# Two small transformers in one kernel: the activation areas of the matmuls placed 64 bytes short of the weight tiles modulo 256, and the low activation product issued last in the second network

## The chip, the cores and the metric

The kernel runs on one core of one Trainium2 chip. The metric is the device time of one execution in microseconds (us); the median of three executions is quoted. One profiled execution gives the trace that all durations come from. The engines in it are TensorE (PE for matmuls, PEld for weight loads), VectorE (DVE), ScalarE (ACT), GpSimd (POOL) and SyncE (SP, which issues the DMAs).

## The reference

Two networks of two layers each are computed one after the other, in fp32, on 256 tokens of 1024 features. The first has 256 more tokens of context, which its first layer carries and its second drops. The second network puts 16 learned tokens in front, so it works on 272.

```
# first network, one layer (cut)
hx = modulate(rmsnorm(x, norm1_g[l]), shift, scale)
p  = hx @ w_in[l]                       # conv branch | q k v | two gates
x  = x + gate * gated_merge(p[..., QKV_END:], conv_branch(...), attention(...), w_out[l])
x  = x + gate * conv_ffn(modulate(rmsnorm(x, norm2_g[l]), ...), w_up[l], ffn_dw[l], ffn_dw_b[l], w_down[l])
# second network, one layer (cut)
u = rmsnorm_2(h, norm_mix[l]);  proj = u @ w_in[l]
h = h + concatenate([a_out, b_out, c_out]) @ w_out[l]      # sparse, differential and retention attention
u = rmsnorm_2(h, norm_ff[l]);   h = h + square(relu(u @ w_ff1[l])) @ w_ff2[l]
```

## The kernel before

All activations live in SBUF, features on the 128 partitions and tokens along the free axis. Every weight is read from HBM once, as a stream of 442 slabs of 128 x 1024 numbers (512 KB). A slab holds 8 tiles of 128 x 128.

**A weight's way.** SP loads slab i into `raw`, a ring of four (`RING`); ScalarE rounds it to fp32r into `w_hi` (line 846); GpSimd writes the rest, raw minus `w_hi`, into `w_lo` in two halves (line 803). SP may load slab i+4 once `w_lo` of slab i is written; ScalarE may round slab i+4 once TensorE has finished slab i. The first network uses `w_hi0`/`w_lo0`, the second `w_hi1`/`w_lo1` over the same bytes; in the second, each pair of tiles starts 64 bytes further than the one before (`TURN` = 16 numbers), so tile k starts 64k bytes further modulo 256.

**A product.** An fp32 product is made of three fp32r matmuls for each tile: high weights by high activations (line 1369), high weights by low activations (line 1370), low weights by high activations (line 1374). The weights are the stationary operand, loaded by a LDWEIGHTS of 128 columns before every matmul, and the activations (`h`, `y`, `at`, `cv`, `fa`, `dn` in the first network; `v`, `u`, `o`, `f` in the second, each as a `_hi` and a `_lo` area) are the moving one: 512 columns in the first layer, 256 in the second layer of the first network, 272 or 256 in the second network. A slab is 24 such matmuls. In `chunk` and in the up projection of the first network all 16 products with `w_hi` come first and the 8 with `w_lo` after them; in the second network the order is high-high, high-low, low-high for each tile. Some products have the weights as the moving operand (lines 1657 to 1659, 1966 to 1968 and 2081 to 2083; two runs of 256 columns each).

**Where the areas start.** The weight tiles start at byte 32896 of a partition. The table gives the start of the moving area relative to that, modulo 256, and how it goes on from one 128-feature tile k to the next.

| area | before | of tile k |
|---|---|---|
| `h`, `y`, `at`, `cv`, `dn` | 0 | same for all k, as are the weights |
| `as`, `cs` (second layer's `at`, `cv`), `fa` | 192 | same for all k, as are the weights |
| `v`, `u`, `o`, `f` with 272 columns | 192, high and low alike | 64k further, as are the weights |
| `u` of the second layer, 256 of its columns (the first 16 left out) | 64 | 64k further, as are the weights |
| `o` of the second layer, 256 columns | 192 | 64k further, as are the weights |

**The up projection of the second layer of the first network** matters below. Its 22 pairs of slabs (`up`, lines 1067, 1752 and 2612) run in loops on all engines. For pair j TensorE makes the `a` chunk and the `g` chunk; ScalarE scales each out of its bank (`up_a`, `up_g`, line 1088), VectorE adds two taps to each (line 2258), ScalarE takes a tanh (`up_t`, line 1093), VectorE makes the product and puts it back into the bank of the `g` chunk (line 2250), ScalarE rounds that into `fa_hi` (line 856) and VectorE writes the rest to `fa_lo`. Between these ScalarE rounds the coming weight slabs. TensorE may write the bank of `g` chunk j only when `fa_lo` of pair j-2 is written (`up_split`).

Of the kernel before, what the change touches and what calls it, by code (L numbers as in the profile page):

```python
# [18 lines left out]
F32 = mybir.dt.float32  # L19
# [93 lines left out]
_n = 0  # L113
for _name, _w in (("ident", P), ("ones_d", P), ("ones_c", P), ("ones_h", P), ("perm1", P), ("perm2", P),
                  ("sel", 8), ("hsel", 16), ("sums", 2), ("cos1", SEQ), ("sin1", SEQ), ("win", GRID_W),
                  ("cos2", T2), ("sin2", T2), ("causal", N1 + N2), ("decay", 4 * 512),
                  ("onehot", VLEN), ("vmask", VLEN)):
    TAB[_name] = (_n, _n + _w)
    _n += _w
# [7 lines left out]
def build(nc, A, out, marks):  # L127
# [44 lines left out]
    with ctx:  # L172
# [28 lines left out]
        w_lo = [weight_area(f"w_lo{n}", w_at + w_size, turn) for n, turn in enumerate((0, TURN))]  # L201
        cst = sb("cst", [6 * P + 26])
        prm = sb("prm", [DEPTH, PRM1_N])
# [67 lines left out]

        def shifted(name, rows, o, by):
            return at(name, [rows, T_BOTH], F32R, o + by)[:, :, 0:SEQ]
# [20 lines left out]
        assert 192 + 3 * DC * T2 * 4 + 4096 <= 2 * DC * T_BOTH * 4  # L294
        tab2 = at("tab2", [2 * T2 + N1 + N2 + 4 * 512], F32, x_at)
# [13 lines left out]
        o_hi = at("o_hi", [DC, T2], F32R, o)  # L309
        o_lo = at("o_lo", [DC, T2], F32R, o + DC * T2 * 4)  # L310
        v_lo = at("v_lo", [DC, T2], F32R, o)
        v_hi = at("v_hi", [DC, T2], F32R, o + DC * T2 * 4)
        units = [(o_hi, o_lo), tuple(at(f"o_{part}1", [DC, T2], F32R, o + 192 + n * DC * T2 * 4) for n, part in enumerate(("hi", "lo")))]
        o += 2 * DC * T2 * 4 + 192
        bias2 = at("bias2", [A_HEADS + B_HEADS, S_ALL], F32, o)
# [6 lines left out]
        assert o + 1536 + 3 * T2 * 4 <= end1, (o, end1)  # L322
        assert g_at + 192 + 2 * FF2_C * T2 * 4 <= o

# [17 lines left out]
        ident = cst[:, 0:P]  # L342
        ones_d, ones_c, ones_h = (cst[:, i * P:(i + 1) * P] for i in (1, 2, 3))
        perm1, perm2, sel = cst[:, 4 * P:5 * P], cst[:, 5 * P:6 * P], cst[:, 6 * P:6 * P + 8]
        hsel = cst[:, 6 * P + 8:6 * P + 24]
        sums = cst[:, 6 * P + 24:6 * P + 26]

# [486 lines left out]
        def _(act):  # L834
# [90 lines left out]
            def network1(layer):  # L925
# [27 lines left out]
                def attend(kind, n, *others):  # L953
# [32 lines left out]
                    elif kind == "mean":  # L986
                        for c in range(CONV_C):
                            act.wait_ge(*after("conv_centred", (layer, c)))
                            act.activation(conv_sq(c)[:, 0:T], cv[:, c, 0:T], ACT.Square).then_inc(*done("ln_sq", (layer, c)))
                    elif kind == "V":  # L990
                        act.wait_ge(*after("attn_pv", (layer, n)))
                        copy(attns[layer][0][:, n, 0:T], aux[3][:, 0:T]).then_inc(*done("attn_hi", (layer, n)))
                    elif kind == "var":

                        ahead(s + 2 * DC)
# [48 lines left out]
                for c in range(CONV_C + 1):  # L1044
# [3 lines left out]
                    if c:  # L1048
                        act.wait_ge(*after("conv_silu", (layer, c - 1)))
                        copy(convs[layer][0][:, c - 1, 0:T], nb[:, c - 1, 0:T]).then_inc(*done("conv_hi", (layer, c - 1)))  # L1050

# [294 lines left out]
        def _(pe):  # L1346
# [29 lines left out]
            def three(o, i, k, a_hi, a_lo, start, stop):  # L1376

                two(o, i, k, a_hi, a_lo, start)
                return third(o, i, k, a_hi, stop)

            def chunk(i, b, T, a_hi, a_lo, key, reader, h_key=None, t0=0):
# [4 lines left out]
                for k in range(DC):  # L1386
                    if h_key:
                        pe.wait_ge(*after("norm_lo", (h_key, k)))
                    two(bank[b][:, t0:T], i, k, a_hi[:, k, t0:T], a_lo[:, k, t0:T], k == 0)
                    if not late:  # L1390
                        mm = third(bank[b][:, t0:T], i, k, a_hi[:, k, t0:T], k == DC - 1)
                if late:
# [201 lines left out]
            def network1(layer):  # L1594
# [108 lines left out]
                def attention_branch(m):  # L1703
# [4 lines left out]
                    for k in range(4):  # L1708
                        three(bank[m % 4][:, 0:T], s + m, 4 + k, attns[layer][0][:, k, 0:T], attns[layer][1][:, k, 0:T], k == 0, k == 3)

                def conv_branch(m):
                    b = 4 + m % 4
                    claim(b)
                    for k in range(4):
                        if m == 0:
                            pe.wait_ge(*after("conv_lo", (layer, k)))
                        mm = three(bank[b][:, 0:T], s + m, k, convs[layer][0][:, k, 0:T], convs[layer][1][:, k, 0:T], k == 0, k == 3)
                    mm.then_inc(*done("slab_used", s + m))
# [529 lines left out]
        def _(dve):  # L2248
# [137 lines left out]
            def network1(layer):  # L2386
# [106 lines left out]
                def rest(p):  # L2493

                    dve.wait_ge(*after("attn_hi", (layer, p)))
                    tt(attns[layer][1][:, p, 0:T], aux[3][:, 0:T], attns[layer][0][:, p, 0:T].bitcast(F32), ALU.subtract)\
                        .then_inc(*done("attn_lo", (layer, p)))
# [51 lines left out]
                for c in range(CONV_C + 2):  # L2549
# [10 lines left out]
                    if c >= 2:  # L2560
                        dve.wait_ge(*after("conv_hi", (layer, c - 2)))
                        tt(convs[layer][1][:, c - 2, 0:T], nb[:, c - 2, 0:T], convs[layer][0][:, c - 2, 0:T].bitcast(F32), ALU.subtract)\
                            .then_inc(*done("conv_lo", (layer, c - 2)))
# [446 lines left out]
def shape_tables():  # L3010
# [9 lines left out]
    put("ones_c", np.full((P, P), 1 / (CONV_C * P)))  # L3020
    put("ones_h", (i[:, None] // HD == i[None, :] // HD) / HD)
    for name, half in (("perm1", 16), ("perm2", 32)):
# [190 lines left out]
```

## Time and profile before

| | |
|---|---|
| median of three executions | 1959.35 us (1958.83 to 1960.12) |
| span of the profiled execution | 1959.9 us |
| TensorE matmuls | 1904.2 us busy (97%), 12126 of them |
| weight loads | 1624.1 us busy (83%) |
| GpSimd | 1187.7 us (61%) |
| VectorE | 1065.5 us (54%) |
| ScalarE | 891.8 us (46%) |
| DMA | 307.04 MB, mean 157 GB/s |
| granted TensorE clock | 9 of 10 tenths or more in all 40 slices |

The span runs from the first to the last instruction. A matmul's duration in the records (277 to 400 ns) is longer than the distance to the next one's start, since they are pipelined: the time that a stream of matmuls takes is read from start to start. Times of rows below are in us from the span's start unless marked ns.

### The profile page before, as it was taken

Reading aid. Unit: us, or ns where it says so; the run is one execution under the profiler, and the core shown is the slowest. Engines: PE = TensorE matmul, PEld = TensorE weight load, DVE = VectorE, ACT = ScalarE, POOL = GpSimd, SP = SyncE. Lnnn points to the kernel's source line nnn. Section 1 sums busy time; section 2 is a strip of 40 time slices with the busy share of each in tenths; the row PEclk is TensorE's granted clock in tenths of the full one; section 3 lists DMA queues with packets and bytes.
Section 4 is the critical chain, followed back from the end, with each engine's and each line's share of the span. In section 5 each row is a group of like instructions: output and inputs, shape, how many; then the busy total and the mean of one; then the engine's idle time right before and its main releaser. Section 6 shows DMA issues by size and latency. Waiting matters only on the chain.

```text
span 1959.9 us, 33261 instructions
## 1 busy us (share of the span) xinstructions
PE 1904.2 (97%) x12126; PEld 1624.1 (83%) x12126; DVE 1065.5 (54%) x1972; ACT 891.8 (46%) x1520; POOL 1187.7 (61%) x904
## 2 busy tenths in 40 slices
PE   7999999999999999999899999999999999999998
PEld 4677777888888887877889999787999998769987
DVE  4899865354443324887657744876542048555400
ACT  4223444243443323525546645556554355555533
POOL 2444233424654554635469987674788876649986
PEclk9999999999999999999999999999999999999999
DMA  9942233628433343436465575432455564326554
GB/s 387 362 127 76 56 96 117 228 78 172 147 107 107 120 149 121 150 91 211 139 204 172 182 230 182 164 108 89 130 183 182 173 206 139 109 75 205 185 179 130
DMA packets 121541, 307.04 MB, mean 157 GB/s; under 512 B 29640, under 2 KB 51528, under 8 KB 121044
## 3 DMA queue, kind: packets, MB, share of 16 engines
q1 hardware_dynamic: 118808, 300.98, 46.8%
q10 hardware_dynamic: 2620, 4.51, 1.5%
q8 instruction: 77, 1.26, 0.3%
q14 instruction: 36, 0.29, 0.0%
HBM read 300.72 MB, written 8.06 MB: 158 GB/s over the span
## 4 chain that ended last, share of the span: by engine, by line
issue 36%; POOL 31%; PE 28%; DVE 4%; ACT 1%; POOLq 0%; ACTq 0%; DVEq 0%
POOL w_lo L803 30%; PE bank L1369 7%; PE bank L1374 6%; PE bank L1370 6%; PE bank L2081 2%; PE bank L2082 2%; PE bank L2083 2%; DVE nb L2258 1%; PE bank L1966 1%; PE bank L1968 1%; PE bank L1967 1%; ACT w_hi L846 0%; DVE v_lo L2258 0%; PE bank L2185 0%; DVE v_lo L2250 0%
## 5 line engine op out<-in xcount | busy, mean ns | idle before, releaser
L803 POOL TENSOR_TENSOR w_lo<-raw,w_hi 128x512 fp32r<-128x512 f32 x884 | 1169.7, 1353 | 759.4 <-ACT w_hi L846 757.2
L846 ACT ACTIVATE w_hi<-raw 128x1024 fp32r<-128x1024 f32 x442 | 466.1, 1056 | 285.2 <-PE bank L1374 146.8
L1369 PE MATMUL bank<-h_hi,w_hi 128*128 128x256 f32 (+1 forms) x1248 | 407.4, 342 | 1.8 <-DVE h_lo L2258 1.1
L1370 PE MATMUL bank<-h_lo,w_hi 128*128 128x256 f32 (+1 forms) x1248 | 399.4, 336 | 0.0
L1369 PEld LDWEIGHTS bank<-h_hi,w_hi 128*128 128x128 f32 x1248 | 237.2, 190 | 43.0 <-issue 13.2
L1374 PE MATMUL bank<-h_hi,w_lo 128*128 128x256 f32 (+1 forms) x1248 | 262.8, 335 | 0.0
L1370 PEld LDWEIGHTS bank<-h_lo,w_hi 128*128 128x128 f32 x1248 | 237.3, 190 | 23.6 <-issue 0.2
L1374 PEld LDWEIGHTS bank<-h_hi,w_lo 128*128 128x128 f32 x1248 | 204.7, 190 | 23.9
L1369 PE MATMUL bank<-u_hi,w_hi 128*128 128x272 f32 (+1 forms) x736 | 212.0, 288 | 1.1 <-DVE u_lo L2258 1.1
L1374 PE MATMUL bank<-u_hi,w_lo 128*128 128x272 f32 (+1 forms) x736 | 209.1, 284 | 0.0
L1370 PE MATMUL bank<-u_lo,w_hi 128*128 128x272 f32 (+1 forms) x736 | 208.3, 283 | 0.0
L1369 PEld LDWEIGHTS bank<-u_hi,w_hi 128*128 128x128 f32 x736 | 138.7, 188 | 5.5 <-issue 3.6
L1370 PEld LDWEIGHTS bank<-u_lo,w_hi 128*128 128x128 f32 x736 | 138.9, 189 | 0.1
L1374 PEld LDWEIGHTS bank<-u_hi,w_lo 128*128 128x128 f32 x736 | 138.9, 189 | 0.0
L2258 DVE SCALAR_TENSOR_TENSOR cv<-upad,prm,cv 128x512 f32<-128x512 f32 x120 | 129.0, 1075 | 3.6
L2258 DVE SCALAR_TENSOR_TENSOR up_g<-bank,prm,up_g 128x510 f32<-128x510 f32 (+1 forms) x88 | 54.2, 616 | 82.4 <-ACT up_g L1088 76.3
L2258 DVE SCALAR_TENSOR_TENSOR up_a<-bank,prm,up_a 128x510 f32<-128x510 f32 (+1 forms) x88 | 54.1, 614 | 56.4 <-ACT up_a L1088 50.4
L2250 DVE TENSOR_TENSOR bank<-bank,sq 128x272 f32<-128x272 f32 (+1 forms) x76 | 33.4, 440 | 93.3 <-ACT up_t L1296 93.2
L1369 PE MATMUL bank<-f_hi,w_hi 128*128 128x272 f32 x256 | 73.8, 288 | 0.0
L1374 PE MATMUL bank<-f_hi,w_lo 128*128 128x272 f32 x256 | 73.8, 288 | 0.0
L2258 DVE SCALAR_TENSOR_TENSOR X<-bank,gh,X 128x256 f32<-128x256 f32 x48 | 21.6, 479 | 95.3 <-PE bank L1374 95.3
L1370 PE MATMUL bank<-f_lo,w_hi 128*128 128x272 f32 x256 | 72.9, 285 | 0.0
(394 smaller groups left out, 3720.8 us busy)
## 6 DMA issues: line engine op xcount, KB each, us to landing
raw<-in_wstream SPq DMA_DIRECT2D x442, 512.0 KB, 3.5
ada_raw<-in_wada SPq DMA_DIRECT2D x48, 512.0 KB, 13.1
late_a<-in_wada SPq DMA_DIRECT2D x16, 512.0 KB, 5.1
late_b<-in_wada SPq DMA_DIRECT2D x16, 512.0 KB, 4.5
biash<-rpb_by_offset SPq DMA_DIRECT2D x64, 64.0 KB, 2.5
gates<-in_wada SPq DMA_DIRECT2D x8, 512.0 KB, 5.0
rpb_by_offset<-in_rpb SPq DMA_DIRECT2D x16, 224.0 KB
bias_by_distance<-vec ACTq DMA_DIRECT2D x1, 3264.0 KB
```

Of the source, the lines that this page charges most:

```text
L803: i = pool.tensor_tensor(lo[:, part, s, :], whole[:, part, :], hi[:, part, s, :].bitcast(F32), ALU.subtract)
L846: act.activation(w_hi[q >= first["l2", 0]][:, :, s, :], raw[:, s, :].rearrange("p (g c) -> p g c", c=PAIR), ACT.Copy)\
L1369: pe.matmul(o, tile(w_hi, i, k), a_hi, start=start, stop=False)
L1370: pe.matmul(o, tile(w_hi, i, k), a_lo, start=False, stop=False)
L1374: return pe.matmul(o, tile(w_lo, i, k), a_hi, start=False, stop=stop)
L1966: pe.matmul(lin[b][:, :], a, wh, start=kk == 0, stop=False)
L1967: pe.matmul(lin[b][:, :], al, wh, start=False, stop=False)
L2081: pe.matmul(o[:, :], hi, wh, start=j == 0, stop=False)
L2082: pe.matmul(o[:, :], lo, wh, start=False, stop=False)
L2083: return pe.matmul(o[:, :], hi, wl, start=False, stop=j == FF2_C - 1)
L2250: return dve.tensor_tensor(o, a, b, op)
L2258: return dve.scalar_tensor_tensor(out=o, in0=a, scalar=s, in1=b, op0=op0, op1=op1)
```

## The change

The activation areas are placed so that they start 64 bytes short of the weight tiles modulo 256 (192 in the table above). `h`, `y`, `at` and `cv` move from 0 to 192; `fa`, and the second layer's `at` and `cv`, which had shifted copies for it, stay at 192. `dn` stays at 0. In the second network the high areas stay at 192 (`u` of the second layer moves so that the 256 columns start at 192 and the 272 at 128), and every low area starts 64 bytes further than its high one, at 0. There the three products of a tile come as high-high, low-high, high-low. An unused table of constants (`ones_h`, 512 bytes of a partition) goes, which makes room. `qT`, `kT`, `gates`, `ada_raw`, `pj` and `V2`, which lie in the same bytes or behind them, move along by 192 bytes modulo 256.

```diff
@@
         X = sb("X", [DC, T_BOTH])
+        top[0] += (w_at - 64 - top[0]) % 256
         h_at = top[0]
@@
-        fa_hi = at("fa_hi", [FF_C, SEQ], F32R, g_at + 192)
-        fa_lo = at("fa_lo", [FF_C, SEQ], F32R, g_at + 192 + FF_C * SEQ * 4)
+        fa_hi = at("fa_hi", [FF_C, SEQ], F32R, g_at)
+        fa_lo = at("fa_lo", [FF_C, SEQ], F32R, g_at + FF_C * SEQ * 4)
@@
-        top[0] += (128 - top[0]) % 256
+        top[0] += (w_at - 64 - top[0]) % 256
         cv_at = top[0]
@@
-        attns = [(at_hi, at_lo), (shifted("as_hi", QC, q_at, 192), shifted("as_lo", QC, q_at + QC * T_BOTH * 4, 192))]
-        convs = [(cv_hi, cv_lo), (shifted("cs_hi", CONV_C, up_at, 192), shifted("cs_lo", CONV_C, cv_at, 192))]
@@
-        o += 192
-        ffn_in = [tuple(at(f"u_{part}{l}", [DC, T2], F32R, o + by + n * DC * T2 * 4) for n, part in enumerate(("hi", "lo")))
-                  for l, by in enumerate((0, -192))]
+        low_part = DC * T2 * 4 + 64
+        ffn_in = [tuple(at(f"u_{part}{l}", [DC, T2], F32R, o + by + n * low_part) for n, part in enumerate(("hi", "lo")))
+                  for l, by in enumerate((0, 192))]
+        o += 256
@@
-        ffn_mid = [tuple(at(f"f_{part}{l}", [FF2_C, n_mid], F32R, o + by + n * FF2_C * n_mid * 4) for n, part in enumerate(("hi", "lo")))
-                   for l, (n_mid, by) in enumerate(((T2, 192), (SEQ, 0)))]
+        ffn_mid = [tuple(at(f"f_{part}{l}", [FF2_C, n_mid], F32R, o + by + n * (FF2_C * n_mid * 4 + 64)) for n, part in enumerate(("hi", "lo")))
+                   for l, (n_mid, by) in enumerate(((T2, 0), (SEQ, 64)))]
@@
             def three(o, i, k, a_hi, a_lo, start, stop):
 
-                two(o, i, k, a_hi, a_lo, start)
-                return third(o, i, k, a_hi, stop)
+                if i < first["l2", 0]:
+                    two(o, i, k, a_hi, a_lo, start)
+                    return third(o, i, k, a_hi, stop)
+                pe.matmul(o, tile(w_hi, i, k), a_hi, start=start, stop=False)
+                pe.matmul(o, tile(w_lo, i, k), a_hi, start=False, stop=False)
+                return pe.matmul(o, tile(w_hi, i, k), a_lo, start=False, stop=stop)
```

The order changes on TensorE alone, in the second network alone. The place below is the end of the first feed-forward projection and the start of the second in its first layer. Before:

```order
L1369 MATMUL bank<-u_hi_111,w_hi_51 128x272
L1370 MATMUL bank<-u_lo_112,w_hi_51 128x272
L1374 MATMUL bank<-u_hi_111,w_lo_53 128x272
L2053 REGISTER_ALU
L2053 COMPARE_AND_BRANCH
L1369 MATMUL bank<-f_hi_123,w_hi_51 128x272
L1370 MATMUL bank<-f_lo_124,w_hi_51 128x272
L1374 MATMUL bank<-f_hi_123,w_lo_53 128x272
```

The same place in the changed kernel:

```order
L1378 MATMUL bank<-u_hi_107,w_hi_51 128x272
L1379 MATMUL bank<-u_hi_107,w_lo_53 128x272
L1380 MATMUL bank<-u_lo_108,w_hi_51 128x272
L2055 REGISTER_ALU
L2055 COMPARE_AND_BRANCH
L1378 MATMUL bank<-f_hi_119,w_hi_51 128x272
L1379 MATMUL bank<-f_hi_119,w_lo_53 128x272
L1380 MATMUL bank<-f_lo_120,w_hi_51 128x272
```

The product with the low activations went from second to third place; nothing was added or taken away.

## Rows read from the trace of the kernel before

**Rows 1.** The page's first section: busy time, share and instructions of each engine.

```profile
PE 1904.2 (97%) x12126; PEld 1624.1 (83%) x12126; DVE 1065.5 (54%) x1972; ACT 891.8 (46%) x1520; POOL 1187.7 (61%) x904
```

**Rows 2.** Groups by line and shape, TensorE: shape, count | busy us, mean ns | idle before.

```profile
L1369 PE MATMUL bank<-h_hi,w_hi 128*128 128x512 f32 x608 | 243.3, 400 | 0.0
...
L1369 PE MATMUL bank<-h_hi,w_hi 128*128 128x256 f32 x640 | 164.2, 287 | 1.8 <-DVE h_lo L2258 1.1 <-ACT V L856 0.8
...
L1369 PE MATMUL bank<-u_hi,w_hi 128*128 128x272 f32 x416 | 121.2, 291 | 0.3 <-DVE u_lo L2258 0.3
...
L1369 PE MATMUL bank<-u_hi,w_hi 128*128 128x256 f32 x320 | 90.9, 284 | 0.8 <-DVE u_lo L2258 0.8
...
L1369 PE MATMUL bank<-f_hi,w_hi 128*128 128x272 f32 x256 | 73.8, 288 | 0.0
```

**Rows 3.** Timeline, TensorE, up projection of layer one: start, duration, what.

```profile
601.73 0.39 PE L1369 MATMUL bank<-h_hi,w_hi 128*128 128x512 f32 x1
...
605.13 0.39 PE L1370 MATMUL bank<-h_lo,w_hi 128*128 128x512 f32 x1
```

**Rows 4.** Timeline, TensorE and VectorE, up projection of layer two, near its end.

```profile
1135.75 0.28 PE L1369 MATMUL bank<-h_hi,w_hi 128*128 128x256 f32 x1
...
1137.43 1.12 PE L1374 MATMUL bank<-h_hi,w_lo 128*128 128x256 f32 x8
1137.46 0.41 DVE L2250 TENSOR_TENSOR fa_lo<-bank,fa_hi 128x256 f32 x1
...
1138.39 0.28 PE L1369 MATMUL bank<-h_hi,w_hi 128*128 128x256 f32 x1
```

**Rows 5.** Timeline, TensorE, attention and convolution outputs of layer two.

```profile
978.02 0.28 PE L1369 MATMUL bank<-as_hi,w_hi 128*128 128x256 f32 x1
...
981.76 0.28 PE L1369 MATMUL bank<-cs_hi,w_hi 128*128 128x256 f32 x1
```

**Rows 6.** Timeline, TensorE, second feed-forward projection of the second network, 272 columns.

```profile
1499.83 0.29 PE L1374 MATMUL bank<-f_hi,w_lo 128*128 128x272 f32 x1
...
1503.18 0.29 PE L1374 MATMUL bank<-f_hi,w_lo 128*128 128x272 f32 x1
```

**Rows 7.** Timeline, TensorE, output projection, last layer, 256 columns.

```profile
1764.94 0.28 PE L1369 MATMUL bank<-o_hi,w_hi 128*128 128x256 f32 x1
...
1767.78 0.28 PE L1369 MATMUL bank<-o_hi,w_hi 128*128 128x256 f32 x1
```

**Rows 8.** Timeline, TensorE, first feed-forward projection, last layer, 256 columns.

```profile
1789.91 0.28 PE L1369 MATMUL bank<-u_hi,w_hi 128*128 128x256 f32 x1
...
1793.07 0.28 PE L1369 MATMUL bank<-u_hi,w_hi 128*128 128x256 f32 x1
```

**Rows 9.** Timeline, TensorE, last feed-forward projection, weights as moving operand.

```profile
1900.18 0.40 PE L2082 MATMUL bank<-w_hi,f_lo 128*128 128x512 f32 x1
1900.42 0.39 PE L2083 MATMUL bank<-w_lo,f_hi 128*128 128x512 f32 x1
...
1904.85 0.40 PE L2081 MATMUL bank<-w_hi,f_hi 128*128 128x512 f32 x1
```

**Rows 10.** Instructions on the tile fa_lo, 1016 to 1150: durations ns, first and last start.

```profile
L2250 DVE TENSOR_TENSOR fa_lo<-bank,fa_hi x21: 411/415/417, 1032.9 to 1148.9; 128x256 f32 x20, 128x256 fp32r<-128x256 f32 x1
```

**Rows 11.** All waits of ScalarE, 1016 to 1147: us in total, times, longest.

```profile
ACT up_t L1093 <- DVE up_g L2258: 26.0, 20, 1.8
ACT fa_hi L856 <- DVE bank L2250: 16.2, 10, 1.8
ACT h_hi L922 <- DVE nb L2258: 3.8, 6, 2.4
ACT up_a L1088 <- PE bank L1374: 3.2, 1, 3.2
```

**Rows 12.** Longest wait of TensorE in the attention of layer two, 800 to 960.

```profile
PE bank L1891 <- DVE sq L2254: 4.5, 6, 1.0
```

More of the change, by code:

```diff
@@ L113 @@
 _n = 0
-for _name, _w in (("ident", P), ("ones_d", P), ("ones_c", P), ("ones_h", P), ("perm1", P), ("perm2", P),
+for _name, _w in (("ident", P), ("ones_d", P), ("ones_c", P), ("perm1", P), ("perm2", P),
                   ("sel", 8), ("hsel", 16), ("sums", 2), ("cos1", SEQ), ("sin1", SEQ), ("win", GRID_W),
@@ L305, in build @@
         V2 = at("V2", [3, 1024], F32, o + L2_FRONT * T2 * 4)
-        ffn_mid = [tuple(at(f"f_{part}{l}", [FF2_C, n_mid], F32R, o + by + n * FF2_C * n_mid * 4) for n, part in enumerate(("hi", "lo")))
-                   for l, (n_mid, by) in enumerate(((T2, 192), (SEQ, 0)))]
+        ffn_mid = [tuple(at(f"f_{part}{l}", [FF2_C, n_mid], F32R, o + by + n * (FF2_C * n_mid * 4 + 64)) for n, part in enumerate(("hi", "lo")))
+                   for l, (n_mid, by) in enumerate(((T2, 0), (SEQ, 64)))]
         o += (L2_FRONT * T2 + 3 * 1024) * 4
[L309 to L314, printed above, removed]
+        o += (w_at - 64 - o) % 256
+        units = [tuple(at(f"o_{part}{l}", [DC, T2], F32R, o + by + n * low_part) for n, part in enumerate(("hi", "lo")))
+                 for l, by in enumerate((0, 192))]
+        v_lo = at("v_lo", [DC, T2], F32R, o + 64)
+        v_hi = at("v_hi", [DC, T2], F32R, o + 256 + DC * T2 * 4)
+        o += 2 * DC * T2 * 4 + 256
         bias2 = at("bias2", [A_HEADS + B_HEADS, S_ALL], F32, o)
@@ L342, in build @@
         ident = cst[:, 0:P]
[L343 to L346, printed above, removed]
+        ones_d, ones_c = (cst[:, i * P:(i + 1) * P] for i in (1, 2))
+        perm1, perm2, sel = cst[:, 3 * P:4 * P], cst[:, 4 * P:5 * P], cst[:, 5 * P:5 * P + 8]
+        hsel = cst[:, 5 * P + 8:5 * P + 24]
+        sums = cst[:, 5 * P + 24:5 * P + 26]
         by_distance = nc.dram_tensor("bias_by_distance", (A_HEADS + B_HEADS, P, VLEN), F32).ap()
@@ L991, in attend @@
                         act.wait_ge(*after("attn_pv", (layer, n)))
-                        copy(attns[layer][0][:, n, 0:T], aux[3][:, 0:T]).then_inc(*done("attn_hi", (layer, n)))
+                        copy(at_hi[:, n, 0:T], aux[3][:, 0:T]).then_inc(*done("attn_hi", (layer, n)))
                     elif kind == "var":
@@ L1049, in network1 @@
                         act.wait_ge(*after("conv_silu", (layer, c - 1)))
-                        copy(convs[layer][0][:, c - 1, 0:T], nb[:, c - 1, 0:T]).then_inc(*done("conv_hi", (layer, c - 1)))
+                        copy(cv_hi[:, c - 1, 0:T], nb[:, c - 1, 0:T]).then_inc(*done("conv_hi", (layer, c - 1)))
                 for m in range(DC):
@@ L1388, in chunk @@
                         pe.wait_ge(*after("norm_lo", (h_key, k)))
-                    two(bank[b][:, t0:T], i, k, a_hi[:, k, t0:T], a_lo[:, k, t0:T], k == 0)
-                    if not late:
-                        mm = third(bank[b][:, t0:T], i, k, a_hi[:, k, t0:T], k == DC - 1)
+                    if late:
+                        two(bank[b][:, t0:T], i, k, a_hi[:, k, t0:T], a_lo[:, k, t0:T], k == 0)
+                    else:
+                        mm = three(bank[b][:, t0:T], i, k, a_hi[:, k, t0:T], a_lo[:, k, t0:T], k == 0, k == DC - 1)
                 if late:
@@ L1708, in attention_branch @@
                     for k in range(4):
-                        three(bank[m % 4][:, 0:T], s + m, 4 + k, attns[layer][0][:, k, 0:T], attns[layer][1][:, k, 0:T], k == 0, k == 3)
+                        three(bank[m % 4][:, 0:T], s + m, 4 + k, at_hi[:, k, 0:T], at_lo[:, k, 0:T], k == 0, k == 3)
                 def conv_branch(m):
@@ L1716, in conv_branch @@
                             pe.wait_ge(*after("conv_lo", (layer, k)))
-                        mm = three(bank[b][:, 0:T], s + m, k, convs[layer][0][:, k, 0:T], convs[layer][1][:, k, 0:T], k == 0, k == 3)
+                        mm = three(bank[b][:, 0:T], s + m, k, cv_hi[:, k, 0:T], cv_lo[:, k, 0:T], k == 0, k == 3)
                     mm.then_inc(*done("slab_used", s + m))
@@ L2495, in rest @@
                     dve.wait_ge(*after("attn_hi", (layer, p)))
-                    tt(attns[layer][1][:, p, 0:T], aux[3][:, 0:T], attns[layer][0][:, p, 0:T].bitcast(F32), ALU.subtract)\
+                    tt(at_lo[:, p, 0:T], aux[3][:, 0:T], at_hi[:, p, 0:T].bitcast(F32), ALU.subtract)\
                         .then_inc(*done("attn_lo", (layer, p)))
```

11 lines of the change are left out of this document (4 added, 7 removed).

## The prediction

> **What bounds the kernel now.** I read the page's first section first [rows 1]: TensorE is busy for 97% of the span and no other engine for more than 61%, so the time is made by the stream of matmuls, and its pace is what counts. Since durations overlap, I then read the pace from start to start, in the timeline, at places where nothing waits:
>
> - 512 columns, `h`: 15 steps from 601.73 to 605.13, 226.7 ns each [rows 3].
> - 256 columns, `h`: 22 steps (14, and then the 8 of the last row but one) from 1135.75 to 1138.39, 120.0 ns each [rows 4].
> - 256 columns, `as` and `cs`: 33 steps from 978.02 to 981.76, 113.3 ns each [rows 5].
> - 272 columns, `f`: 27 steps from 1499.83 to 1503.18, 124.1 ns each [rows 6].
> - 256 columns, `o` of the last layer: 24 steps from 1764.94 to 1767.78, 118.3 ns [rows 7]; `u` of the last layer: 27 steps from 1789.91 to 1793.07, 117.0 ns [rows 8].
>
> Four paces for one size of matmul. `as` and `h` have the same columns, the same row length and the same weights; by the code they differ in where the area starts. What fits all rows is the distance between two streams that run together: while matmul n streams its activation columns, the weights of matmul n+1 are loaded (both engines' rows are busy side by side, 97% and 83% [rows 1]). Let d be the start of those weights minus the start of the streaming activations, modulo 256. One column at the full 2.4 GHz level makes 106.7 ns of 256 columns, so what is paid on top is:
>
> - d = 0 always (`h`): 13.3 ns a matmul.
> - d = 64 always (`as`, `cs`): 6.6 ns.
> - d = 64, 64, 128 (`o`; the third matmul of a tile is followed by the next tile's weights, 64 bytes further): three steps are 354.9 ns, and two of them at 113.3 leave 128.3 for the third, so d = 128 costs 21.6 ns.
> - d = 192, 192, 0 (`u` of the last layer): 117.0 on average.
> - 272 columns (113.3 ns of streaming), d = 64, 64, 128: 10.8 ns on average; by the costs above it would be (6.6 + 6.6 + 21.6) / 3 = 11.6. So the columns hardly matter, the distances do. And 512 columns (213.3 ns) at d = 0 pay 13.4, as 256 do.
>
> **The change part by part.** It makes d = 64 nearly everywhere. The counts are those of line 1369 [rows 2], times three for the three products; smaller groups of the same view are told with their count.
>
> First network, 512 columns: `h` 608, `y` 64, `at` 32, `cv` 32, together 736, or 2208 matmuls. No row has 512 columns with the activations moving at d = 64. The bounds are no gain and 13.4 ns (all that is paid now); I take 6.7, because at d = 0 the cost is the same 13.3 at either width and at 256 columns half of it goes [rows 3 to 5]. 2208 x 6.7 = 14.8 us. `dn` (504 matmuls) stays at 0 and gains nothing.
>
> First network, 256 columns: `h` 640 and `y` 64, or 2112 matmuls, from 120.0 to 113.3: 14.2 us at full price.
>
> Second network, 272 columns: `u` 416 (of which 48 are the second layer's), `f` 256, `v` 120, `o` 64; without those 48 it is 808, or 2424 matmuls. The new order and the 64 bytes of the low areas turn 64, 64, 128 into 64, 64, 64: after low-high come the same tile's high weights, and the last product streams the low area, which starts 64 further, so the next tile's weights are again 64 ahead. The step would be 113.3 + 6.6 = 119.9 against 124.1: 2424 x 4.2 = 10.2 us. Bounds: nothing, and 10.8 ns (26 us).
>
> Second network, 256 columns: `u` 320, or 960 matmuls, from 117.0 to 113.3, 3.6 us; `o` 64, or 192, from 118.3, 1.0 us.
>
> Small ones, taken together as nothing: the second layer's 144 matmuls of `u` with 272 columns get d = 128 throughout where they had 0, 0, 64 (144 x 10 ns, 1.5 us lost); where the weights move (lines 1657, 1966, 2081) the stationary activations shift, and in 128 of them d goes from 0 or 128 to 64 or 192 (about 9 ns each, 1.2 us won). The attention products on `qT`, `kT`, `pj` and `V2` are true fp32 and have no low parts; I count their 192 bytes at nothing, with a loss of 1 us as the far bound. The new order itself costs nothing: `w_lo` was waited for at the start of a chunk before as well, a weight load stands before each matmul either way, and no other engine's order moves. GpSimd, ACT and DMA get 4% less time for a slab in places: all of GpSimd's 1187.7 us over 442 slabs are 2.69 us a slab [rows 1], against 2.72 for 24 steps of 113.3. In the down projection of layer two TensorE already runs at that pace with `fa`.
>
> Sum at full price: 14.8 + 14.2 + 10.2 + 4.6 = 43.8 us.
>
> **What takes its place.** In the up projection of layer two TensorE makes a pair of slabs in 48 x 120.0 = 5.76 us. `fa_lo`, the last step of each pair on the other engines, starts 21 times from 1032.9 to 1148.9: 116.0 / 20 = 5.80 us a pair [rows 10]. That is slower than TensorE, and it isn't TensorE that makes it so: in this stretch ScalarE waits 42.2 us for VectorE and once, at the start, for TensorE [rows 11]. Scaling, taps, tanh, product, rounding and the coming weight slab make a ring of ScalarE and VectorE that turns on its own. TensorE needs `fa_lo` of two pairs back for its bank; near the end that is written at 1137.87 and needed at 1138.39 [rows 4], 0.5 us of slack. Faster matmuls use up the slack and then wait in step with the ring. There 40 slabs x 24 = 960 of the 2112 matmuls lie, worth 6.4 us; 0.5 stays, 5.9 goes.
>
> In the attention of both layers, TensorE waits for the softmax (six times, 4.5 us, in layer two [rows 12]). Of the gate chunks between a pair's scores and its transposes the gain is swallowed by a longer wait: 8 slabs a layer at 24 x 6.7 ns, 1.3 us each, most of it in layer two: 2 us. The starts of stages (norms, the first loads in the first 50 us) take 2 us more, an estimate from the loose steps there. Together 9.9 us are lost of 43.8, and 33.9 us are left. The profiled span is 1959.9, half a us over the median of 1959.35, so nothing lies outside it; the forecast is 1959.35 - 33.9 = **1925.5 us**, 1.7% less.
>
> **A rule that speaks against it.** The rows show one matmul shape at 120.0 and at 113.3 ns with only the area's start changed [rows 4, 5]. The Trainium skill, "SBUF — State Buffer", section "SBUF: two separate sides", says that on the engine side only the pair of ports shared by VectorE and GpSimd causes contention and that TensorE waits for no one; "TensorE: Matmul & The Clock Gate", Part 2, gives the moving operand and the weight load a read port each, so that one takes no bandwidth from the other. By that the start of an area can't matter and the change would be worth nothing.
>
> **The rivals.** (a) Placement isn't the cause, and `as`, `cs` and `fa` are fast for a reason that goes with their stages: 1959, no change. Against it: `f`, `o` and `u` have three more paces, and the distances alone put all of them in order. 4%. (b) At 512 columns the cost doesn't fall, since the load is over halfway through the matmul, and what is paid isn't the meeting of two streams but a start-up: 14.8 less, 1940. For it: no row with 512 at 64. Against it: the equal 13.3 at 256. 12%. (c) The second network keeps 124, because the 64-distance there was never alone: 10.2 less, 1936. 12%, and 2% for (b) and (c) together, 1950. (d) The ring in the up projection isn't as fixed as it looks; its product on VectorE takes 0.4 or 1.4 us, as it meets GpSimd or not, and with other phases it may turn in less than 5.76: up to 5.9 more, and the attention's 2, 1917. 7%. (e) Slower: the 512-column matmuls fall on a worse place instead of a better. With the weights moving, 512-column steps take 233.5 on average (20 steps, 1900.18 to 1904.85) and single ones 240 [rows 9]. Without the 14.8 the rest is worth 19.1; it is gone when the 2208 lose 8.7 ns each, at a step of 235.4. At 240 the sum is 1959 - 19 + 29, so 1969. 3%.
>
> **How the numbers follow.** The forecast case, 1925.5, has 60%; (a) 4, (b) 12, (c) 12, both 2, (d) 7, (e) 3. Its own working bounds are some 5 us either way (the swallowed part, and 1 to 2 ns on 2424 matmuls). To leave out no more than 20% the range takes in (b), (c) and (d): 1914 to 1943. 0.2% (4 us) is about what a measurement of this kernel can tell from no change. Faster by more: all but (a), (e), with a little off for both together: 0.93; within: 0.04; slower: 0.03.
>
> **What would show it.** In the changed kernel's timeline: steps of 220 ns with `h` at 512 columns (226.7 means b); 113.3 with `h` at 256 outside the up projection of layer two; in that stage about 5.8 us a pair, with TensorE waiting for `fa_lo`, and ScalarE still not waiting for TensorE; 120 at 272 columns in a slab of 2.88 us (124 means c); 113.3 for `u` and `o` of the last layer; `dn` still at 227. What would make the prediction wrong is above all the width of 512, 14.8 of the 33.9, and a GpSimd that doesn't keep up at 2.72 us a slab where the ring of four starts empty.

## The result: 0.6% slower, and the profile after

The changed kernel takes 1972.39 us (median of 4 runs, 1970.29 to 1974.56) beside 1959.57 for the kernel before, a ratio of 1.0062 with a 95% interval of 1.0051 to 1.0074. Forecast were 1925.5, and 1943 at most. In a second comparison, ten runs beside nineteen of before, the ratio was 1.0054 (1.0039 to 1.0069). All ratios here compare executions in the chip's usual, faster state; one of an experiment below, 3123.58 us at a mean granted clock of 0.555, is left out by that. The profiled execution spans 1971.2 us where that of before spans 1959.9.

The page's first section and one of its groups. TensorE has 12.7 us more of busy time than in [rows 1], with the same number of instructions; VectorE, ScalarE and GpSimd are within 1.1 us of it:

```profile
PE 1916.9 (97%) x12126; PEld 1623.0 (82%) x12126; DVE 1064.4 (54%) x1972; ACT 891.5 (45%) x1520; POOL 1187.0 (60%) x904
...
L1366 PE MATMUL bank<-h_hi,w_hi 128*128 128x256 f32 (+1 forms) x1248 | 409.0, 344 | 3.6 <-DVE fa_lo L2252 1.7
```

The timeline answers to [rows 3], the up projection of layer one with 512 columns. From 602.02 to 605.29 are 14 steps (4, the 8 low products, 2), 233.6 ns each, where 220 was forecast and 226.7 was before:

```profile
602.02 0.40 PE L1366 MATMUL bank<-h_hi,w_hi 128*128 128x512 f32 x1
...
602.96 2.03 PE L1371 MATMUL bank<-h_hi,w_lo 128*128 128x512 f32 x8
604.82 0.40 PE L1366 MATMUL bank<-h_hi,w_hi 128*128 128x512 f32 x1
605.06 0.39 PE L1367 MATMUL bank<-h_lo,w_hi 128*128 128x512 f32 x1
605.29 0.40 PE L1366 MATMUL bank<-h_hi,w_hi 128*128 128x512 f32 x1
```

Layer two, 256 columns, the same lines and tiles at two places (answers to [rows 4]). From 1059.89 to 1063.89 are 34 steps of 117.6 ns; from 1099.84 to 1100.98 are 10 of 114. In between and behind stand waits for `fa_lo`, and after one of them the other pace is there:

```profile
1059.89 0.28 PE L1366 MATMUL bank<-h_hi,w_hi 128*128 128x256 f32 x1
...
1063.89 0.28 PE L1366 MATMUL bank<-h_hi,w_hi 128*128 128x256 f32 x1
...
1099.84 0.28 PE L1366 MATMUL bank<-h_hi,w_hi 128*128 128x256 f32 x1
...
1100.98 1.07 PE L1371 MATMUL bank<-h_hi,w_lo 128*128 128x256 f32 x8
1102.48 0.39 PE L1366 MATMUL bank<-h_hi,w_hi 128*128 128x256 f32 x1 [0.44 <-DVE fa_lo L2252]
```

The second network, answers to [rows 6] and [rows 8]: 272 columns, 30 steps from 1515.05 to 1518.83, 126.0 ns (124.1 before); `u` of the last layer, 30 steps from 1800.03 to 1803.48, 115.0 ns (117.0 before).

```profile
1515.05 0.29 PE L1378 MATMUL bank<-f_hi,w_hi 128*128 128x272 f32 x1
...
1518.83 0.29 PE L1378 MATMUL bank<-f_hi,w_hi 128*128 128x272 f32 x1
...
1800.03 0.28 PE L1378 MATMUL bank<-u_hi,w_hi 128*128 128x256 f32 x1
...
1803.48 0.28 PE L1378 MATMUL bank<-u_hi,w_hi 128*128 128x256 f32 x1
```

Where the time went is read from the first start of some tiles. The answers for single tiles (durations min/median/max, first and last start), first of before, then of the changed kernel:

```profile
L1369 PE MATMUL bank<-dn_hi,w_hi x168: 387/389/467, 656.1 to 775.2; 128*128 128x512 f32 x168
L1369 PE MATMUL bank<-fa_hi,w_hi x176: 276/276/384, 1147.0 to 1207.1; 128*128 128x256 f32 x176
L1369 PE MATMUL bank<-f_hi,w_hi x256: 287/288/290, 1496.6 to 1591.7; 128*128 128x272 f32 x128
L2081 PE MATMUL bank<-w_hi,f_hi x128: 390/395/478, 1861.4 to 1953.9; 128*128 128x512 f32 x128
```

```profile
L1366 PE MATMUL bank<-dn_hi,w_hi x168: 387/389/467, 666.4 to 785.6; 128*128 128x512 f32 x168
L1366 PE MATMUL bank<-fa_hi,w_hi x176: 276/276/384, 1157.0 to 1218.6; 128*128 128x256 f32 x176
L1378 PE MATMUL bank<-f_hi,w_hi x256: 283/288/289, 1510.1 to 1606.6; 128*128 128x272 f32 x128
L2083 PE MATMUL bank<-w_hi,f_hi x128: 388/395/482, 1872.5 to 1965.1; 128*128 128x512 f32 x128
```

The lag, by which the same instruction starts later in the changed kernel, is 10.3 us at the start of `dn` (nearly all of it 512-column work), 11.5 at the start of `y` in layer two (986.4 and 997.9, rows below), 10.0 at the start of `fa` and 11.5 at its end, 13.5 at the start of `f` and 14.9 at its end, 11.1 at the last projection, 11.3 at the end of the span. So the first 650 us lose nearly all, the rest of the first network loses 1.2 more, the 272-column layer takes 3.4, and the last one gives 3.8.

**The clock has a share in this.** Both traces have short stretches in which TensorE is granted 1.2 GHz, and the changed kernel's has one more, in the attention of layer two, right after TensorE had waited 1.79 us for `qT`. The answer for this stretch (0.50, the third number from the end, is the granted share of the full 2.4 GHz; before has 1.00 in this part):

```profile
827.90:831.30 3.40, 3.40 (x17) 3.31 (x16) 2.65 (x7) 1.69 (x3) 3.40 (x4) 0.50 0.57 163
```

In it 15 matmuls of 256 columns start, where at 117.8 ns there would be 29: 1.6 us of the lag. The mean granted clock of the two profiled executions is 0.994 and 0.991. Over the 82 runs of before on record, 0.001 less of it goes with about 1.2 us more (a straight line through them, an estimate), and the 14 runs of the changed kernel have 0.9937 on average where those have 0.9947. So some 1 to 2 of the 10 to 13 us go with the clock; whether the change brings that about wasn't tested.

### The profile page after: what moved, and what is told of

Same layout as the page of the kernel before. It is cut to its first block, busy times and chain, and to the rows that moved or that the text cites. A ratio compares the mean times of both kernels' runs of the same rounds, so it can differ in the third digit from the quotient of the medians.

```text
span 1971.2 us, 33261 instructions
## 1 busy us (share of the span) xinstructions
PE 1916.9 (97%) x12126; PEld 1623.0 (82%) x12126; DVE 1064.4 (54%) x1972; ACT 891.5 (45%) x1520; POOL 1187.0 (60%) x904
## 4 chain that ended last, share of the span: by engine, by line
issue 37%; POOL 30%; PE 29%; DVE 3%; ACT 1%; POOLq 0%; DMA 0%; ACTq 0%; DVEq 0%
POOL w_lo L800 30%; PE bank L1378 7%; PE bank L1379 6%; PE bank L1380 6%; PE bank L2084 2%; PE bank L2085 2%; PE bank L2083 2%; PE bank L1968 1%; PE bank L1970 1%; PE bank L1969 1%; PE bank L2187 0%; DVE nb L2260 0%; PE bank L1371 0%; DVE v_lo L2252 0%; DVE v_lo L2260 0%
```

## The experiments

**Theories.** T1: 512-column steps are slower at d = 64 than at d = 0 (the prediction's rival e at a smaller price), and that is the loss. T2: it comes from the second network's new order. T3: the low bytes alone don't set the pace; it also depends on the moment at which a stream starts.

**Streams alone.** One source line for each size and distance; before each stream four matmuls of 256 + p columns:

```
for p in (0, 2, 4, 6):
    prelude(p)
    for k in range(32):
        pe.matmul(bank[5][:, 0:256], still(k), moving(256, 64, k), ...)
```

> This kernel leaves out both networks: it only makes streams of 32 matmuls on TensorE, each matmul loading its own 128-column weights from one area and streaming 256, 272 or 512 columns from another, one source line for each size and each distance d (start of the weights minus start of the streamed columns, modulo 256, in steps of 16 bytes), and every stream four times, behind four matmuls of 256, 258, 260 or 262 columns that shift the moment at which it begins. Theory of the prediction (the low byte of the two starts alone sets the pace): each size and distance has one step for all four beginnings; 256 columns about 120 ns at d = 0 and 113.3 at 64, 512 columns 226.7 at one of the distances and 233 at others. Rival (the pace also depends on the moment at which the stream locks in): at 256 columns and d = 64 some beginnings give 113.3 and others 117.7, as the two paces of the changed kernel's own steps. For 512 columns the rival to the prediction's additive term says 233 at d = 64 and 226.7 at d = 0, for every beginning.

The timeline at 256 columns and d = 64, the four beginnings one after the other (L67 is the prelude, L92 the stream; start, duration, what, count):

```profile
103.79 3.81 PE L92 MATMUL bank<-a_flat,w 128*128 128x256 f32 x32
107.44 0.64 PE L67 MATMUL bank<-w 128*128 128x258 f32 x4
107.91 3.80 PE L92 MATMUL bank<-a_flat,w 128*128 128x256 f32 x32
111.55 0.64 PE L67 MATMUL bank<-w 128*128 128x260 f32 x4
112.03 3.93 PE L92 MATMUL bank<-a_flat,w 128*128 128x256 f32 x32
115.80 0.65 PE L67 MATMUL bank<-w 128*128 128x262 f32 x4
116.28 3.93 PE L92 MATMUL bank<-a_flat,w 128*128 128x256 f32 x32
```

The same columns, weights and bytes take 3.8 or 3.93 us, according to the length (256 and 258 columns, or 260 and 262) of the four matmuls that went before. With the starting steps left out that is 113.3 and 117.8 ns, the two paces of the changed kernel. At 512 columns, d = 0 (L232) and d = 64 (L252), two beginnings each:

```profile
594.25 7.42 PE L232 MATMUL bank<-a_flat,w 128*128 128x512 f32 x32
...
601.99 7.44 PE L232 MATMUL bank<-a_flat,w 128*128 128x512 f32 x32
...
720.90 7.62 PE L252 MATMUL bank<-a_flat,w 128*128 128x512 f32 x32
...
728.84 7.63 PE L252 MATMUL bank<-a_flat,w 128*128 128x512 f32 x32
```

Mean steps from start to start, in ns (two numbers: by the beginning):

| d | 256 columns | 272 columns | 512 columns |
|---|---|---|---|
| 0 | 119.8 | 125.2 to 126.5 | 227.5 |
| 32 | 118.4 | 125.3 | 233.3 |
| 64 | 113.9 / 117.8 | 123.5 | 233.3 |
| 96 | 117.4 to 118.7 | 123.7 | 234.2 |
| 112 | 113.4 / 118.6 | 124.7 | 233.0 |
| 128 | 118.6 | 126.5 | 232.3 / 233.5 |
| 144 | 114.5 to 115.1 | 123.5 / 126.5 | 231.1 |
| 192 | 117.9 | 126.7 | 229.1 / 233.4 |

T1 and T3 hold. Of 16 distances, 0 is the best one for 512 columns and the worst but one for 256. For 256 columns d = 144 is the only distance with less than 116 ns behind all four beginnings; no kernel was built on it. The price that the prediction worked out for d = 128 (21.6 ns over 106.7) isn't there: 118.6 is 11.9 over. VectorE, ScalarE and GpSimd do nothing here, so the difference is made within TensorE's own two streams. The Trainium skill ("SBUF — State Buffer", section "SBUF: two separate sides", and "TensorE: Matmul & The Clock Gate", Part 2), which the prediction set against the change, says that TensorE waits for no other engine there and that loading the next weights takes no read bandwidth from the running matmul. That would leave one time for every place, and this trace disagrees: 3.80 and 3.93 us for one stream, 7.42 and 7.62 for 512 columns at two distances. In the map only the streamed columns move; that the distance counts, and not their own place, is shown further down, where the weights move.

**The moment of the start.** The streams follow each other without a pause, with a single matmul of 256 + q columns between them, q = 0, 2, ... 30:

> Leaves out both networks: streams of 48 matmuls follow each other without a pause, each behind a single matmul of 256 + q columns, q from 0 to 30, which pushes the stream to a later start. At 256 columns and distance 64: theory of two locks, set by the moment at which the stream starts: some q give 113.3 for the whole stream, others 117.7, and the same q can give either, as it depends on where the stream before stood. Rival (the beginning doesn't matter, something else picked the step in the first map): all q give one step. At distance 0: 120.0 for every q; 512 columns: 226.7 at distance 0 and 233.3 at 64 for every q.

A piece of the timeline at 256 columns and d = 64 (48 matmuls in a stream):

```profile
52.64 0.28 PE L80 MATMUL bank<-w 128*128 128x262 f32 x1
52.76 5.61 PE L82 MATMUL bank<-a_flat,w 128*128 128x256 f32 x48
58.21 0.28 PE L83 MATMUL bank<-w 128*128 128x264 f32 x1
58.33 5.82 PE L85 MATMUL bank<-a_flat,w 128*128 128x256 f32 x48
...
75.65 5.61 PE L94 MATMUL bank<-a_flat,w 128*128 128x256 f32 x48
```

Nine of the sixteen q give 5.60 to 5.62 us, seven 5.82, with nothing between; the second pass over all q repeats the same sixteen answers. A stream keeps its pace to its end once it has it (T3). At d = 0 the four q tried are all at 120.0 after a few steps, and 512 columns at 226.7 (d = 0) and 233.3 (d = 64) for the four q tried.

**Each network alone.** The new places of the first network only, and the places and the order of the second only; the low bytes of the other network's areas are those of before.

```
# first network only: the second one's areas back to their low bytes
-        low_part = DC * T2 * 4 + 64
+        low_part = DC * T2 * 4
...
-                if i < first["l2", 0]:
-                    two(o, i, k, a_hi, a_lo, start)
```

> The kernel before with the new places of the first network alone; the second network has the low bytes and the order of before. If the 512-column steps cause the loss (2208 of them at 233.4 in place of 226.7 ns, +14.8 us, against some 2 to 6 us won at 256 columns), this is slower than before by 9 to 13 us: 1969 to 1973 us. If the loss came from the second network, it is at or below 1959, by the prediction's sum 1939.

> The kernel before with the new places and the new order of the second network alone. If the first network causes all of the loss, this is within 3 us of before (272-column steps of 124.3 became about 126, +3 us; the 256-column ones of the last layer 1 ns less, -1 us): 1958 to 1963. By the prediction's sum it would be 1945 (11.8 of 13.8 us won). If the second network caused the loss, 1970.

> The changed kernel itself, beside the runs of before on this chip, to put the two halves and the whole on one scale: the halves alone cost 7.1 and 1.6 us. If they add up, 8.7 us, 1968; if they hinder each other, 12 us as in its first runs, 1972.

Measured: the first network alone 1967.12 us, ratio 1.0036 (1.0019 to 1.0054), 7 us slower; the second alone 1961.35, 1.0008 (0.9998 to 1.0019). The whole change on the same chip 1970.23, 10.1 over before. So most of the loss is the first network's, and T2 explains at most the small part; with intervals of 2 to 3 us either way I can't say whether the halves (8.7 us) add up to the whole (10.6 by its ratio) or cost more together.

The kernel with the first network alone shows by the way that the places don't fix which of the two paces comes. Up to here its program has the same matmuls at the same low bytes as the changed kernel. The answers for `y_hi` from 900 to 1100 us, of before, of the changed kernel, and of this one:

```profile
L1369 PE MATMUL bank<-y_hi,w_hi x64: 278/283/387, 986.4 to 1009.3; 128*128 128x256 f32 x64
```

```profile
L1366 PE MATMUL bank<-y_hi,w_hi x64: 281/281/388, 997.9 to 1020.3; 128*128 128x256 f32 x64
```

```profile
L1366 PE MATMUL bank<-y_hi,w_hi x64: 276/276/383, 997.7 to 1019.6; 128*128 128x256 f32 x64
```

A median of 281 ns goes with steps of 117.8, one of 276 with 113.3: the same stage has the slow pace in one kernel and, for the first 120 of its 192 matmuls, the fast one in the other. It doesn't take another kernel. The changed kernel was profiled twice, and at the start of the up projection of layer two its products with `h_hi` have the slow pace in the first execution and the fast one in the second, from nearly the same moment:

```profile
L1366 PE MATMUL bank<-h_hi,w_hi x32: 281/281/471, 1030.3 to 1041.4; 128*128 128x256 f32 x32
L1366 PE MATMUL bank<-h_hi,w_hi x32: 276/276/467, 1030.4 to 1041.1; 128*128 128x256 f32 x32
```

**The second network's places without its order.**

> As the kernel with the second network's part alone, but with the order of before (high by high, high by low, low by high) while the low activations still lie 64 bytes further. The prediction's additive rule says: low activations now stand at d = 0 against the next weights, low weights of the same tile, and cost more than the new order, 1950 to 1955; theory that the order makes no difference: the same time as that kernel within 1.5 us; theory that the new order is what made the 272-column steps 126: 1 to 3 us faster than that kernel.

1962.23 us, 1.0016 (1.0007 to 1.0026): the same as with the order, within the noise. Its 272-column steps are 125.0, so both the place and the order had made something worse, and neither paid.

**The second network's order, streams alone.** Tiles and activations advance by 64 bytes from row to row, as in the kernel:

```
def new(n, d, low, turn):
    ... high weights x high, low weights x high, high weights x low (low further by `low`)
```

> Leaves out both networks: TensorE runs streams of 48 matmuls alone, in the networks' own orders (high by high, high by low, low by high; the order of the changed kernel; and the first network's, with the low weights behind) and with the second network's steps of 64 bytes from row to row of both weights and activations, one source line for each order, size, distance of the high activations (steps of 32 bytes) and place of the low ones (level or 64 bytes further), each behind three beginnings. Theory of the prediction (the sum of a price for each distance): 272 columns at distance 64 give 124.5 in the old order and 123.5 or less in the new one with the low activations 64 bytes further. Rival (the bare stream shows what the changed kernel showed): 126 to 127 in the new order with the low activations further, 124.3 in the old one with them level, so the distance between two starts isn't enough to tell the step. For 512 columns both say 227 at distance 0 and 233 at 64.

272 columns, d = 64: the old order with level low areas (L174), the new one with the low areas 64 further (L270), 48 matmuls each:

```profile
512.99 6.13 PE L174 MATMUL bank<-a_flat,w 128*128 128x272 f32 x48
...
979.96 6.20 PE L270 MATMUL bank<-a_flat,w 128*128 128x272 f32 x48
```

124.4 and 125.8 ns: the bare streams show what these kernels show (124.1 and 126.0), and 115.5 for the last layer's new arrangement where its old one has 117.0 (before and the changed kernel: 117.0 and 115.0). All three neighbours of the new order are at d = 64, where a stream at a fixed place has 123.5. So the distance between neighbours isn't enough; what else counts when the places advance stays open. Of the 32 arrangements of 272 columns tried, two (d = 96, low areas level, in either order) have 122.9 behind one of their three beginnings and 125.0 behind the other two; no other stream is below 124.3, and the kernel before, at 124.4 behind all three, was as good as any that keeps its pace.

**The 512-column steps alone.** The weight tiles lie 192 bytes earlier (d = 64) while the part with 512 columns runs, and then move to their old place; no activation area changes its low byte.

```
+        w_hi.append(weight_area("w_hi2", w_at - 192, 0))
+        def view(i):
+            return 1 if i >= first["l2", 0] else 0 if i >= further else 2
```

> The kernel before with its weight tiles 192 bytes earlier, distance 64, in the part of the first network that has the 512-column matmuls (layer one, and layer two up to its values), and everything else at the distances of before. 2712 matmuls of 512 columns (the 504 of the down projection too) go from distance 0 to 64, and 480 of 256 columns with them. Theory (512 columns cost 6.7 ns more at 64): +18.2 us, less 1 to 3 us for the 256-column ones, so 1974 to 1977 us and a down projection of 124 us where before has 120.7. The prediction's rule (6.7 ns less): 1941. If the loss of the changed kernel has another cause than the 512-column step: 1959.

1970.91 us, 1.0064 (1.0047 to 1.0081): 11.5 us slower at the medians, from the 512-column steps; beside them only three slabs wait for their room a slab longer, which in the next experiment, with the same wait, costs nothing that can be measured. `dn`, which the change had left at 227, now goes at 233.3 (six pairs in 2.80 us):

```profile
700.04 0.40 PE L1378 MATMUL bank<-dn_hi,w_hi 128*128 128x512 f32 x1
...
702.84 0.40 PE L1378 MATMUL bank<-dn_hi,w_hi 128*128 128x512 f32 x1
```

T1 is shown, with its sign and its price per step, and so is that the distance makes it: the weights moved and the activations didn't. The whole came out 3 to 6 us lower than expected, and part of that lies ahead of `dn`: its first start is 665.3, 9.2 us later than before, where 2112 steps by 6.7 make 14.1. The first start of `y` in layer one tells where: it is 364.3 for 361.5, so the 960 steps ahead of it, 6.4 us by the price, show up as 2.8. From there to `dn` the price holds: 1152 steps by 6.7 less 1.3 for 192 matmuls of 256 columns are 6.4, and the lag grows by 6.4. What took up 3.6 us in the first 361 stays open. The four runs also had a little more clock than before (0.9958 for 0.9950 on average), some 1 us by the estimate above.

**The 256-column steps alone.** The same means the other way round: from the first gate slab of layer two on, the weight tiles are 64 bytes further, and everything with 512 columns stays at d = 0.

> The kernel before, with the distance 64 made from the other side: from the first gate slab of the first network's second layer on, the weight tiles lie 64 bytes further, and every activation area of that part stands level with them as before (the attention, convolution and feed-forward areas lose their shift of 192). All 512-column matmuls keep distance 0. If the loss of the changed kernel is that of its 512-column steps, and only the distance counts, the 672 matmuls of 256 columns outside the rings go from 120 to between 113.3 and 117.7 ns: 1.5 to 4.5 us won, 1955 to 1958 for 1959.5. If the gain at 256 columns needs the activations to be moved, no change: 1959.5. If the three slabs that wait one slab longer for their room cost more than that, 1961.

1960.30 us, 1.0003 (0.9990 to 1.0017). The steps did get shorter (`y` at 117.8, `h` in the gates and the up projection at 113.3 or 117.8 for 120.0), but the 192 of `y` only got the smaller gain, and some of the rest ended in longer waits: TensorE's idle time ahead of the high products of 256 columns went from 1.8 to 4.8 us [rows 2]:

```profile
L1377 PE MATMUL bank<-h_hi,w_hi 128*128 128x256 f32 x640 | 161.3, 285 | 4.8 <-DVE fa_lo L2258 1.9 <-ACT V L864 1.8 <-DVE h_lo L2266 1.0
```

**A kernel that beats both.** Two pieces: the changed kernel's order and places in the last layer alone (115.0 for 117.0 ns), and the last stage, where 512 columns of weights are streamed, with both operands level:

```
+        w_hi.append(weight_area("w_hi2", w_at + 192, 0))
-                   for l, (n_mid, by) in enumerate(((T2, 192), (SEQ, 0)))]
+                   for l, (n_mid, by) in enumerate(((T2, 192), (SEQ, 192)))]
```

> The kernel before with the changed kernel's order and places in the second network's last layer alone (low activations 64 bytes further and last of the three products), where the second map has 115.5 for 117.0 ns at 256 columns; the 272-column layer stays as before at 124.4. 960 matmuls of the feed-forward input by 1.5 ns and 192 of the units by 0.8: 1.6 us faster, 1957.9 for 1959.5, if TensorE sets the pace there. If what it waits for there comes no earlier: 1959.5. If the new order itself costs something in a kernel that the bare streams don't show: 1961.

> The kernel before, with the last stage alone changed: the last 29 weight slabs lie without the 64-byte step from row to row, 192 bytes into the weight areas, and the activations that are loaded against them (the feed-forward middle of the last layer) at the same low byte. There 512 columns of weights are streamed past stationary activations, 233.5 ns a step before. Theory (512 columns are at their fastest at distance 0, whatever of the two is streamed): 348 matmuls by 6.5 ns, 2.3 us faster, 1957.1 for 1959.4, with steps of 227 in the last 90 us. Rival: the fast step at distance 0 belongs to streamed activations, or the jump between two rows within one stream decides: steps stay at 229 to 238, no change, 1959.4. If the three slabs that wait one slab longer for room hold TensorE up: 1960.

> That and the changed kernel's order and places in the last layer of the second network together. By the sum of steps 2.3 and 1.6 us: 3.9 us faster than before, 1955.5 for 1959.4; if only one of the two comes, 1957 to 1958.

The first alone: 1958.25, 0.9993 (0.9984 to 1.0003). The second alone: 1958.76, 1.0000 (0.9991 to 1.0010), which can't tell 2.3 us from nothing, but its trace can for the stage. The answers for `f_lo` in the last stage, of before and of this kernel, have 92.4 us from the first start to the last and 90.3:

```profile
L2082 PE MATMUL bank<-w_hi,f_lo x128: 389/394/402, 1861.7 to 1954.1; 128*128 128x512 f32 x128
```

```profile
L2095 PE MATMUL bank<-w_hi,f_lo x128: 387/389/403, 1855.8 to 1946.1; 128*128 128x512 f32 x128
```

Both together: **1956.09 us, 0.9981 (0.9972 to 0.9991)**, 3.6 us faster than before. Its steps in the last stage answer to [rows 9], 21 of them in 4.76 us, 226.7 ns for 233.5:

```profile
1900.14 0.39 PE L2100 MATMUL bank<-w_hi,f_hi 128*128 128x512 f32 x1
...
1904.90 0.39 PE L2100 MATMUL bank<-w_hi,f_hi 128*128 128x512 f32 x1
```

So d = 0 is the fast place at 512 columns whichever operand is streamed, even where the stream jumps between two rows half way.

The other piece is less certain. In the kernel with the last stage alone the first feed-forward projection of the last layer has the order and the places of before, and its `u` goes at another pace than in [rows 8]: 27 steps in 3.08 us, 114.1 ns for 117.0 (over the whole projection 113.9, as in the kernel with the first network alone).

```profile
1789.99 0.28 PE L1382 MATMUL bank<-u_hi,w_hi 128*128 128x256 f32 x1
...
1793.07 0.28 PE L1382 MATMUL bank<-u_hi,w_hi 128*128 128x256 f32 x1
```

So the old arrangement has two paces too, 117 in three traces and 113.9 in two, and the new one's 115.0, in all five of its traces, is better than the first and worse than the second. How often each comes without the profiler isn't known; the 3.6 us are measured, their split between the two pieces isn't.

## Why the prediction was wrong

- **512 columns, the step that failed.** The prediction gave them 6.7 ns less, "because at d = 0 the cost is the same 13.3 at either width and at 256 columns half of it goes", with no loss as the bound. It is 6.9 more in the row shown (233.6; 6.7 in the bare streams): 2208 x 6.9 = 15.2 us lost by the steps where 14.8 were to be won, 30 of the 47 us between forecast and result. What failed is the inference: a price read at 256 columns was carried over to 512, with no row for it, and the term's bounds (no gain, 13.4) left no room for a loss. The equal 13.3 was a coincidence of two sizes at one distance. Rival (e) named the mechanism and its chance was too small (3%); it asked for a loss of 8.7 ns a step to decide, but that sum held all the other gains in full.
- **256 columns of the first network.** 113.3 was forecast, and 113.3 or 117.8 came, by the moment at which a stretch of matmuls begins. The row at 113.3 [rows 5] was one of two paces of that place. A stretch at the slower one gets 2.2 of the 6.7 ns. Which of the two came in [rows 5] was luck: in the changed kernel's trace the attention's output at the same distance has 117.8.
- **The ring of the up projection: right.** `fa_lo` starts 21 times from 1043.8 to 1159.8 in the changed kernel, 5.80 us a pair as in [rows 10], and TensorE now waits for it (1.7 us, five times). So 960 of the 2112 matmuls gained next to nothing, as forecast:

```profile
L2252 DVE TENSOR_TENSOR fa_lo<-bank,fa_hi x21: 411/415/416, 1043.8 to 1159.8; 128x256 f32 x20, 128x256 fp32r<-128x256 f32 x1
```

- **272 columns, the second step that failed.** 124.1 should have become 119.9 and became 126.0: 2424 x 1.9 = 4.6 us lost where 10.2 were to be won. It rested on adding prices of single distances, of which the one for d = 128 had been solved from one mean of three steps [rows 7]. The map has no such price.
- **Last layer, 256 columns.** Right in sign beside this trace of before, 2.0 of 3.7 ns for `u` (1.9 us); beside the old arrangement's other pace (113.9) it would be a loss of 1.1.
- **The swallowed part** was about right in size. The lag at `y` of layer two (11.5) stands beside 15.2 by the steps, less the 1 to 3 us that 480 matmuls of 256 columns won, and 1.6 of it is the clock's: 2 to 4 us were taken up, where the forecast had 4 outside the ring. By the rows of the 512-column experiment most of it went in the first 361 us.
- The order of views was sound: TensorE's pace did make the time, and nearly all of the loss is in it, with 1 to 2 us that go with the clock, which no term and no rival had. Wrong was a model with as many prices as rows. It fitted six paces and had no row left to be tested on.

## What to carry over

Before areas are moved for the sake of TensorE's step, run the kernel's own sequence of matmuls alone, at every place on offer and behind several beginnings: 1.7 ms of bare streams gave the signs of the 512- and the 272-column parts of this change, and the paces of its traces to 1 ns. They didn't give all: the 113.9 of the old `u` came in two kernels and behind none of the three beginnings. A price read at one width doesn't hold at another (here d = 0, nearly the worst place at 256 columns, is the best at 512), and a step read at one place may be one of two, so read it in two profiled executions before a sum rests on it. Read the granted clock of both traces beside any difference of a few microseconds. With 512 columns, try both operands at the same byte modulo 256 first: it was the fast place in each case here.

## What the runs showed of the hardware

- At 256 columns and d = 64 a run of matmuls settles at 113.3 or 117.8 ns and stays there; two more columns in one matmul ahead of it are enough to change which (d = 112 shows 113.4 and 118.6).
- At 512 columns, d = 0 alone of 16 distances (multiples of 16 bytes) gives 226.7 ns; the others have 229 to 237. The changed kernel's steps there alternate, 231 and 236.
- The pace at one place differs between kernels that are alike up to it (`y`, 276 and 281 ns of duration), and between two executions of one kernel (`h`, 276 and 281), so a stage can move by a microsecond or two with nothing changed in it.
- TensorE's granted clock falls to 1.2 GHz for a few stretches of a kernel that is 97% busy, one of them right behind a wait of 1.79 us, and their number differs between executions: the runs of before have a mean of 0.992 to 0.999.
